# Three layer norms: the modulated activations made on VectorE, their high parts on ScalarE, and three instructions moved

## The chip, the cores and the metric

The kernel runs on one core of one Trainium2 chip. A core has TensorE (PE, matmuls), VectorE (DVE, elementwise), ScalarE (ACT, one-input functions with a scale and a bias for each partition), GpSimd (POOL, which here mostly issues DMAs) and SyncE (SP, DMAs only). The engines run their own instruction streams and wait for each other by semaphores. The metric is device time of one execution in microseconds (us), the median of the runs shown.

## The reference, cut to what matters

The whole computation is two transformer blocks, one after the other, for 512 tokens of width 1024. The first has an attention layer and a gated linear attention layer, each with an MLP. The second has a gated delta net and a retention layer, each followed by a convolutional feed-forward net (FFN). The change touches the second one only, where each of the four sublayers ends in a layer norm:

```
def _standardize(x, eps):
    mu = jnp.mean(xf, axis=-1, keepdims=True)
    xc = xf - mu
    var = jnp.mean(xc * xc, axis=-1, keepdims=True)
    return xc * lax.rsqrt(var + eps)

for i in range(DEPTH):                       # DEPTH = 2
    sh1, sc1, g1, sh2, sc2, g2 = jnp.split(mod, 6, axis=-1)
    y = mixers[i % N_MIXERS_2](x * (1.0 + sc1) + sh1)
    x = layer_norm(DN_ALPHA * x + (1.0 + g1) * y, ln_g[i, 0], ln_b[i, 0])
    y = conv_ffn(x * (1.0 + sc2) + sh2, ffn_up[i], ffn_conv_w[i], ffn_conv_b[i], ffn_down[i])
    x = layer_norm(DN_ALPHA * x + (1.0 + g2) * y, ln_g[i, 1], ln_b[i, 1])
```

What the next product reads is h = x * (1 + sc) + sh, and x itself is normed times gain plus bias. So h is the normed value times one column of numbers plus another, one number of each for every feature.

## The kernel before, in words

Activations lie transposed: `xT[:, b, 256:768]` is block b (0 to 7) of 128 features for the 512 tokens. Large matmuls are done in float32 accuracy from split operands: a value is cut into a rounded high part (fp32r) and the rest, its low part, and a product is three matmuls, high x high, low x high and high x low (`split_product`, L737 records all of them). ACT makes the high parts by writing them in fp32r. DVE makes the low parts by subtraction: `w_lo` for weights (L2335, in two halves of a group), `x_lo` for activations (L2341 and L2344).

The four layer norms are named ln0 (after the delta net), ln0f (after FFN 0), ln1 (after retention) and ln1f (after FFN 1, the last work before the output). Each has two pieces.

- `add_residual` runs over the eight output blocks j of the projection ahead of the norm, as PE finishes them. DVE adds each block to `xT`, centres it around a first mean, and adds the squares that ACT makes (`ln_squares`, L1931) to a sum (`add_squares`, L2715). Between them stand splits of weights: the lists `before` and `after` say behind which block a group is split. At j = 6 it is the group `ffn0_up` 0 for ln0, `ffn1_up` 0 for ln1, and for ln0f and ln1f the last group of the FFN's own down projection, which PE still needs for block 7 (it takes this group from the 12th of its 22 steps on). ACT does the high half of the same group just ahead of squares 6 and 7.
- `layer_norm` follows once the sums over features are there. PE adds up over the partitions by matmuls with ones: `begin_sums` (L796, L798) stands six matmuls ahead of the end of block 7 and takes squares 0 to 6, `end_sums` (L803, L805) takes block 7. ACT makes the reciprocal deviation (`ln_deviation`, L1940 and L1942, semaphore n_std). DVE centres each block once more (`center`, L2763) and multiplies it by the deviation (L2778, semaphore n_mul). For ln0, ln0f and ln1, ACT then makes h in `hT` (L1588) and copies it to its high part (L1561 for ln0 and ln1, which write an array with holes, L1563 for ln0f), and DVE subtracts for the low part (L2341 or L2344), two blocks behind its multiplications. For ln1f there is no next product: ACT applies gain and bias (L1596).

PE's next stage goes block by block over the same eight inputs: for input block k it waits for low part k (`input_split`), then does six matmuls. The first such column of 48 matmuls needs weight group 0, the next one group 1, whose high parts ACT makes behind its last activation of the norm (for ln0 and ln1 behind a load of its function table too), and whose low parts DVE makes behind its last x_lo.

After ln0 there is more. POOL streams the modulation weights `in_ada_w` for the last norms in pieces of 256 KB. Its loop waits for n_mul to reach 40, which is the eighth multiplication of ln0, since a slot of the pieces lies in the deviation's array. DVE weighs four pieces (`mod_piece`, L2163 and L2165) ahead of its split of group 1 of `ffn0_up`, and four behind it.

The order on each engine is that of the code: no planner moves anything. SP loads weight groups into a ring of two slots, each as soon as PE has begun on the group after the one in the slot.

## Time and profile before

| | |
|---|---|
| median of 3 runs | 3748.09 us |
| lowest, highest | 3744.73, 3749.03 us |
| the profiled execution: time, span | 3753.23 us, 3751.5 us |
| PE busy | 3512.0 us, 94% of the span |
| PE weight loads busy | 2820.2 us, 75% |
| DVE busy | 1917.2 us, 51% |
| ACT busy | 1194.3 us, 32% |
| POOL busy | 211.6 us, 6% |
| mean granted TensorE clock | 0.973 of full speed |

Times of rows count from the start of the span. The span is the profiled execution on the core, 1.7 us less than its time. The busy share is an average over some forty stages, so it says that PE is the engine to look at, not what a norm costs. For that one reads the four stretches in which PE waits for a norm or starts the column behind it: about 2463 to 2489 us (ln0), 2863 to 2888 (ln0f), 3339 to 3362 (ln1) and 3726 to 3741 (ln1f).

### The profile page before, as it was taken

Reading aid. Unit: us, or ns where it says so; the run is one execution under the profiler, and the core shown is the slowest. Engines: PE = TensorE matmul, PEld = TensorE weight load, DVE = VectorE, ACT = ScalarE, POOL = GpSimd, SP = SyncE. Lnnn points to the kernel's source line nnn. Section 1 sums busy time; section 2 is a strip of 40 time slices with the busy share of each in tenths; the row PEclk is TensorE's granted clock in tenths of the full one; section 3 lists DMA queues with packets and bytes.
Section 4 is the critical chain, followed back from the end, with each engine's and each line's share of the span. In section 5 each row is a group of like instructions: output and inputs, shape, how many; then the busy total and the mean of one; then the engine's idle time right before and its main releaser. Section 6 shows DMA issues by size and latency. Waiting matters only on the chain.

```text
span 3751.5 us, 45103 instructions
## 1 busy us (share of the span) xinstructions
PE 3512.0 (94%) x17014; PEld 2820.2 (75%) x17014; DVE 1917.2 (51%) x2755; ACT 1194.3 (32%) x1545; POOL 211.6 (6%) x374
## 2 busy tenths in 40 slices
PE   7999889999997998899999999789998999899998
PEld 3566679999995887677846665678877777678876
DVE  4555546445446564644445665577745333454434
ACT  3033424213224342533322333243323222333332
POOL 0111001001000000111100000011100000000000
PEclk9999999999998999999999999899999999999999
DMA  6212114234221111444421111045533222122222
GB/s 209 80 58 65 49 36 133 93 99 127 91 85 41 40 56 56 135 157 154 157 68 35 34 34 45 23 140 181 181 108 101 67 73 73 56 84 96 89 84 84
DMA packets 294723, 335.30 MB, mean 89 GB/s; under 512 B 16465, under 2 KB 264145, under 8 KB 294481
## 3 DMA queue, kind: packets, MB, share of 16 engines
q1 hardware_dynamic: 261552, 232.93, 19.7%
q0 software_dynamic: 29440, 96.49, 8.1%
q10 hardware_dynamic: 3617, 4.26, 0.4%
q8 instruction: 83, 1.36, 0.2%
q14 instruction: 31, 0.25, 0.0%
HBM read 331.55 MB, written 2.10 MB: 89 GB/s over the span
## 4 chain that ended last, share of the span: by engine, by line
PE 86%; DVE 6%; ACT 2%; DMA 2%; issue 2%; ACTq 0%; DVEq 0%; POOL 0%; SPq 0%; POOLq 0%
PE acc L737 64%; PE sc L737 6%; PE sc L1318 2%; DMA wring<-in_mlp_w 1%; PE acc L962 1%; PE sc L878 1%; PE sc L942 1%; PE acc L1318 1%; PE acc L1498 1%; PE sc L944 1%; DVE w_lo L2335 1%; DVE arena L2093 1%; DVE xT L2097 0%; DVE d_col L2284 0%; PE acc L953 0%
## 5 line engine op out<-in xcount | busy, mean ns | idle before, releaser
L737 PE MATMUL acc<-x_lo,w_hi 128*128 128x512 f32 (+1 forms) x2144 | 810.1, 378 | 31.3 <-DVE d_out_lo L2312 9.2
L2335 DVE TENSOR_TENSOR w_lo<-wring,w_hi 128x1024 fp32r<-128x1024 f32 (+2 forms) x400 | 441.7, 1146 | 560.1 <-ACT w_hi L1674 560.1
L1674 ACT ACTIVATE w_hi<-wring 128x1024 fp32r<-128x1024 f32 (+2 forms) x400 | 377.4, 991 | 996.6 <-DMA wring<-in_mlp_w 483.1
L737 PEld LDWEIGHTS acc<-x_lo,w_hi 128*128 128x128 f32 x2144 | 408.5, 191 | 95.4 <-DVE w_lo L2335 25.4
L737 PE MATMUL acc<-hid_hi,w_hi 128*128 128x512 f32 (+1 forms) x1120 | 415.0, 371 | 18.6 <-DVE w_lo L2335 9.3
L737 PE MATMUL acc<-hid_hi,w_lo 128*128 128x512 f32 (+1 forms) x1120 | 410.7, 367 | 0.0
L737 PE MATMUL acc<-x_hi_holes,w_hi 128*128 128x512 f32 x704 | 282.1, 401 | 15.3 <-DVE x_lo L2341 13.9
L737 PE MATMUL acc<-x_hi_holes,w_lo 128*128 128x512 f32 x704 | 278.5, 396 | 0.0
L737 PE MATMUL acc<-hid_lo,w_hi 128*128 128x384 f32 (+1 forms) x768 | 272.2, 354 | 0.0
L737 PEld LDWEIGHTS acc<-hid_hi,w_hi 128*128 128x128 f32 x1120 | 212.0, 189 | 48.0 <-DVE arena L2371 11.8
L737 PE MATMUL acc<-x_hi_seq,w_hi 128*128 128x512 f32 x576 | 228.1, 396 | 16.2 <-DVE x_lo L2344 13.7
L737 PEld LDWEIGHTS acc<-hid_hi,w_lo 128*128 128x128 f32 x1120 | 211.8, 189 | 24.8
L737 PE MATMUL acc<-x_hi_seq,w_lo 128*128 128x512 f32 x576 | 225.2, 391 | 0.0
L737 PE MATMUL acc<-x_hi,w_hi 128*128 128x384 f32 (+1 forms) x608 | 208.6, 343 | 11.2 <-DVE x_lo L2344 6.2
L737 PE MATMUL acc<-x_hi,w_lo 128*128 128x384 f32 (+1 forms) x608 | 207.4, 341 | 0.0
L737 PE MATMUL acc<-wide_lo,w_hi 128*128 128x512 f32 x480 | 188.6, 393 | 0.0
L737 PE MATMUL sc<-hT,wring 128*128 128x512 f32 x384 | 177.7, 606 | 0.5 <-DVE d_col L2561 0.5
L723 POOL DMA_DIRECT2D rows_or_mod<-in_ada_w x176 | 94.9, 539 | 1421.3 <-DVE xT L2778 605.0
L737 PEld LDWEIGHTS acc<-x_hi_holes,w_hi 128*128 128x128 f32 x704 | 133.5, 190 | 48.1 <-issue 16.1
L2165 DVE SCALAR_TENSOR_TENSOR tab<-rows_or_mod,cs,tab 128x512 f32<-128x512 f32 x204 | 147.9, 748 | 30.8 <-DMA rows_or_mod<-in_ada_w 27.4
L737 PEld LDWEIGHTS acc<-x_hi_holes,w_lo 128*128 128x128 f32 x704 | 133.6, 190 | 32.5
L737 PEld LDWEIGHTS acc<-hid_lo,w_hi 128*128 128x128 f32 x768 | 145.0, 189 | 9.8
(416 smaller groups left out, 5930.7 us busy)
## 6 DMA issues: line engine op xcount, KB each, us to landing
wring<-in_mlp_w SPq DMA_DIRECT2D x64, 1024.0 KB, 5.4
rows_or_mod<-in_ada_w POOLq DMA_DIRECT2D x208, 256.0 KB, 3.1
wring<-in_ffn_up SPq DMA_DIRECT2D x44, 1024.0 KB, 5.1
wring<-in_ret_w_in SPq DMA_DIRECT2D x24, 1024.0 KB, 5.2
rstd<-in_ada_w POOLq DMA_DIRECT2D x88, 256.0 KB, 3.4
wring<-in_ffn_down SPq DMA_DIRECT2D x32, 704.0 KB, 4.7
wring<-in_gdn_w_in SPq DMA_DIRECT2D x16, 1024.0 KB, 5.8
tab<-in_ada_w POOLq DMA_DIRECT2D x40, 256.0 KB, 3.4
```

What stands on the lines that cost most here:

```text
L723: pool.dma_start(mod_w[s], w[:, k, bass.ds(it * (per * MOD_N) + i * MOD_N, MOD_N)]).then_inc(mod_loaded[s], 16)
L737: ins = pe.matmul(o, lhsT, rhs, start=start, stop=stop)
L878: last = pe.matmul(mod_psum[:, bass.ds(it * (MOD_PIECES[phase] // DB * per * nv) + c, 1)], mod_acc[:, i % 2, v, m * P:(m + 1) * P], ones[: ...
L942: pe.matmul(sc[:, n % 2, h, 0:w], qn[:, e, t * P:(t + 1) * P], kn[:, e, k0:k0 + w], start=True, stop=False)
L944: last = pe.matmul(sc[:, n % 2, h, 0:w], qr[:, t * P:(t + 1) * P], krope[:, e, k0:k0 + w], start=False, stop=True)
L962: last = pe.matmul(unit(S, 11 + 2 * n)[:, 0, 0:P], vtok[:, k, e * P:(e + 1) * P], probT[:, n % 2, k * P:(k + 1) * P], start=k == 0, stop=k ...
L1318: last = pe.matmul(o[:, e, t], left[:, e, t], right[:, e, t], start=True, stop=True)
L1498: last = pe.matmul(unit(S, 8 + j)[:, i, t * P:SEQ], r_v[:, t, m // CTX, m % CTX:m % CTX + P], r_s[:, t, 0:SEQ - t * P], start=t == 0, stop ...
L1674: f(w_hi[s][:, c], wring[s][:, c], ACT.Copy).then_inc(w_high, 1)
L2093: st.did(tt(y[:, b + 1], y[:, b + 1], rstd[:, 0:n], MUL))
L2165: ins = stt(a, mod_w[s], cs[:, k, v:v + 1], a, MUL, ADD)
L2335: tt(w_lo[s][:, c], wring[s][:, c], w_hi[s][:, c].bitcast(F32), SUB).then_inc(w_split, 1)
```

## The change

Three edits.

1. In `add_residual` at j = 6 the sum takes square 6 (the seventh) ahead of the split of the next weights, in all four norms, where it stood behind it.
2. In `layer_norm` each multiplication stands ahead of the centring of the block three further on, where it stood behind it.
3. For ln0, ln0f and ln1, ACT writes the high part of h from `xT` in one activation with scale and bias, and no longer `hT`. DVE computes `hT` itself by a tensor_scalar (times one column, plus another), one for each block, and subtracts for the low part one block behind, where it was two. The tensor_scalar waits for n_mul, DVE's own multiplication, and the subtraction for h_ready, DVE's own tensor_scalar, besides x_high.

```
--- before.py
+++ after.py
@@ -1585,9 +1585,9 @@
 
                 for b in range(DB):
                     act.wait_ge(n_mul, mul0 + b + 1)
-                    f(hT[:, b, CTX:T], xT[:, b, CTX:T], ACT.Identity, scale=ln_col[:, i, 0, b:b + 1],
-                      bias=ln_col[:, i, 1, b:b + 1]).then_inc(h_ready, 1)
-                    high_input(SEQ, b, h0, holes)
+                    x = xT[:, b, CTX:T]
+                    f(x_hole(b) if holes else x_hi_seq[:, b, :], in_two(x) if holes else x, ACT.Identity,
+                      scale=ln_col[:, i, 0, b:b + 1], bias=ln_col[:, i, 1, b:b + 1]).then_inc(x_high, 1)
 
             def layer_norm_out(l, i, mul0):
 
@@ -2334,9 +2334,13 @@
                     dve.wait_ge(w_high, half_group(stage, it, j, h))
                     tt(w_lo[s][:, c], wring[s][:, c], w_hi[s][:, c].bitcast(F32), SUB).then_inc(w_split, 1)
 
-            def low_input(n, b, x0, holes=False):
+            H0 = 40
+
+            def low_input(n, b, x0, holes=False, h0=None):
 
                 dve.wait_ge(x_high, x0 + b + 1)
+                if h0 is not None:
+                    dve.wait_ge(h_ready, h0 + b + 1)
                 if holes:
                     tt(in_two(x_lo[:, b, CTX:T]), in_two(hT[:, b, CTX:T]), x_hole(b).bitcast(F32), SUB).then_inc(x_split, 1)
                     return
@@ -2745,11 +2749,11 @@
                             st.did(ins)
                         else:
                             ins.then_inc(x_added, 1)
-                    for b in {3: (1,), 4: (2,), 5: (3,), 6: (5,)}.get(j, ()):
+                    for b in {3: (1,), 4: (2,), 5: (3,), 6: (5, 6)}.get(j, ()):
                         add_squares(b)
                     splits(after.get(j, ()))
-                    for b in {5: (4,), 6: (6,)}.get(j, ()):
-                        add_squares(b)
+                    if j == 5:
+                        add_squares(4)
                     if phase and j == 5:
                         dve.wait_ge(mod_summed, 1 + MOD_CHUNKS * (phase + 1))
                         modulation(phase + 1, 0, 6, 1)
@@ -2758,6 +2762,7 @@
             def layer_norm(name, i, x0=None, holes=False, follows=None):
 
                 _, b0, _ = NORMS[name]
+                h0 = H0 + DB * i
 
                 def center(b):
                     st.did(stt(xT[:, b, CTX:T], sc[:, 0, 1, :], -1.0 / D, xT[:, b, CTX:T], MUL, ADD))
@@ -2771,16 +2776,21 @@
                 if follows:
                     split_weights(*follows)
                 deviation_of(name)
+                if x0 is not None:
+                    dve.wait_ge(ln_cols, (1, 3, 3)[i])
                 for b in range(DB):
+                    st.settle(min(2, DB - 1 - b))
+                    tt(xT[:, b, CTX:T], xT[:, b, CTX:T], rstd[:, 0:SEQ], MUL).then_inc(n_mul, 1)
                     if b + 3 < DB:
                         center(b + 3)
-                    st.settle(min(3, DB - 1 - b))
-                    tt(xT[:, b, CTX:T], xT[:, b, CTX:T], rstd[:, 0:SEQ], MUL).then_inc(n_mul, 1)
-                    if x0 is not None and b >= 2:
-                        low_input(SEQ, b - 2, x0, holes)
+                    if x0 is not None:
+                        dve.wait_ge(n_mul, 8 * (4 + i) + b + 1)
+                        ts(hT[:, b, CTX:T], xT[:, b, CTX:T], ln_col[:, i, 0, b:b + 1], ln_col[:, i, 1, b:b + 1],
+                           MUL, ADD).then_inc(h_ready, 1)
+                        if b:
+                            low_input(SEQ, b - 1, x0, holes, h0)
                 if x0 is not None:
-                    low_input(SEQ, DB - 2, x0, holes)
-                    low_input(SEQ, DB - 1, x0, holes)
+                    low_input(SEQ, DB - 1, x0, holes, h0)
 
             def down_residual(i, l, x0):
```

DVE's stream at the end of `add_residual` of ln0f, before. L2715 adds a square to the sum (the one with `rstd` square 5, the other square 6), L2335 splits the last weight group of the down projection (128x704, two halves):

```order
L2743 TENSOR_TENSOR sq<-sq,xT 128x512 [waits dve_step]
L2715 TENSOR_TENSOR sq<-sq,rstd 128x512 [waits n_used,n_sq]
L2335 TENSOR_TENSOR w_lo<-wring,w_hi 128x704 [waits w_high] x2
L2715 TENSOR_TENSOR sq<-sq 128x512 [waits n_used,n_sq]
L2728 SCALAR_TENSOR_TENSOR xT<-acc,dcol,xT 128x512 [waits acc_ready,n_cent]
```

The same place in the changed kernel (line numbers are a few higher):

```order
L2747 TENSOR_TENSOR sq<-sq,xT 128x512 [waits dve_step]
L2719 TENSOR_TENSOR sq<-sq,rstd 128x512 [waits n_used,n_sq]
L2719 TENSOR_TENSOR sq<-sq 128x512 [waits n_used,n_sq]
L2335 TENSOR_TENSOR w_lo<-wring,w_hi 128x704 [waits w_high] x2
L2732 SCALAR_TENSOR_TENSOR xT<-acc,dcol,xT 128x512 [waits acc_ready,n_cent]
```

The add of square 6 with its wait for n_sq, ACT's square, now stands in front of both halves of the split.

DVE's stream at the start of `layer_norm` of ln0, before, from the centrings of blocks 0 to 2 on. L2763 centres, L2778 multiplies, L2341 makes a low part:

```order
L2763 SCALAR_TENSOR_TENSOR xT<-sc,xT 128x512 x3
L2763 SCALAR_TENSOR_TENSOR xT<-sc,xT 128x512 [waits n_std]
L2778 TENSOR_TENSOR xT<-xT,rstd 128x512 [waits dve_step]
L2763 SCALAR_TENSOR_TENSOR xT<-sc,xT 128x512
L2778 TENSOR_TENSOR xT<-xT,rstd 128x512 [waits dve_step]
L2763 SCALAR_TENSOR_TENSOR xT<-sc,xT 128x512
L2778 TENSOR_TENSOR xT<-xT,rstd 128x512 [waits dve_step]
L2341 TENSOR_TENSOR x_lo<-hT,x_hi_holes 128x512 [waits x_high]
```

In the changed kernel L2768 centres, L2783 multiplies, L2788 is the new tensor_scalar and L2345 makes a low part:

```order
L2768 SCALAR_TENSOR_TENSOR xT<-sc,xT 128x512 x3
L2783 TENSOR_TENSOR xT<-xT,rstd 128x512 [waits dve_step,ln_cols,n_std]
L2768 SCALAR_TENSOR_TENSOR xT<-sc,xT 128x512
L2788 TENSOR_SCALAR hT<-xT,ln_col 128x512 [waits n_mul]
L2783 TENSOR_TENSOR xT<-xT,rstd 128x512 [waits dve_step]
L2768 SCALAR_TENSOR_TENSOR xT<-sc,xT 128x512
L2788 TENSOR_SCALAR hT<-xT,ln_col 128x512 [waits n_mul]
L2345 TENSOR_TENSOR x_lo<-hT,x_hi_holes 128x512 [waits h_ready,x_high]
```

Ahead of the first multiplication stand three centrings instead of four. Ahead of the first low part stand five centrings, two multiplications and two tensor_scalars, where there were six centrings and three multiplications.

The end of the same norm and what follows it on DVE, before. The low parts 5, 6 and 7 stand behind the last multiplication; L2163 and L2165 weigh modulation pieces, and `w_lo1` is group 1 of `ffn0_up`:

```order
L2778 TENSOR_TENSOR xT<-xT,rstd 128x512 [waits dve_step]
L2341 TENSOR_TENSOR x_lo<-hT,x_hi_holes 128x512 [waits x_high] x3
L2844 MEMSET sq 128x2x2
L2832 UNCONDITIONAL_BRANCH
L2832 ISA
L2159 ISA [waits mod_summed]
L2163 TENSOR_SCALAR tab<-rows_or_mod,cs 128x512 [waits mod_loaded0]
```

And in the changed kernel, from the seventh multiplication on:

```order
L2783 TENSOR_TENSOR xT<-xT,rstd 128x512 [waits dve_step]
L2788 TENSOR_SCALAR hT<-xT,ln_col 128x512 [waits n_mul]
L2345 TENSOR_TENSOR x_lo<-hT,x_hi_holes 128x512 [waits h_ready,x_high]
L2783 TENSOR_TENSOR xT<-xT,rstd 128x512 [waits dve_step]
L2788 TENSOR_SCALAR hT<-xT,ln_col 128x512 [waits n_mul]
L2345 TENSOR_TENSOR x_lo<-hT,x_hi_holes 128x512 [waits h_ready,x_high] x2
L2854 MEMSET sq 128x2x2
```

The last multiplication now has six low parts and seven tensor_scalars in front of it, where it had five low parts. The streams of PE, SP and POOL are the same in both kernels. ACT's loses the second of its two activations for each of 24 blocks.

## Rows read from the trace of the kernel before

**Rows 1.** The page's part on the chain that ended last, shares of the span.
```profile
PE 86%; DVE 6%; ACT 2%; DMA 2%; issue 2%; ACTq 0%; DVEq 0%; POOL 0%; SPq 0%; POOLq 0%
```
**Rows 2.** Timeline of DVE, ln0: start us, length us, engine, line, operation.
```profile
2457.35 0.68 DVE L2715 TENSOR_TENSOR sq<-sq,rstd 128x512 f32<-128x512 f32 x1
...
2469.52 0.68 DVE L2778 TENSOR_TENSOR xT<-xT,rstd 128x512 f32<-128x512 f32 x1
...
2472.52 0.68 DVE L2341 TENSOR_TENSOR x_lo<-hT,x_hi_holes 128x512 fp32r<-128x512 f32 x1
...
2479.14 0.68 DVE L2778 TENSOR_TENSOR xT<-xT,rstd 128x512 f32<-128x512 f32 x1
...
2487.41 2.36 DVE L2335 TENSOR_TENSOR w_lo<-wring,w_hi 128x1024 fp32r<-128x1024 f32 x2
```
**Rows 3.** Timeline of ACT, ln0.
```profile
2457.13 0.61 ACT L1931 ACTIVATE sq<-xT 128x512 f32<-128x512 f32 x1
...
2470.30 0.81 ACT L1588 ACTIVATE hT<-xT,ln_col 128x512 f32<-128x512 f32 x1 [1.67 <-DVE xT L2778]
```
**Rows 4.** Timeline of PE, ln0; in brackets the idle time and its releaser.
```profile
2459.25 1.02 PE L796 MATMUL sc<-sq,base_tab 128*128 128x512 f32 x2
2460.96 1.12 PE L798 MATMUL sc<-sq,base_tab 128*128 128x512 f32 x2 [0.69 <-DVE sq L2715]
...
2473.35 0.77 PE L737 MATMUL acc<-x_hi_holes,w_hi 128*128 128x512 f32 x1 [6.96 <-DVE x_lo L2341]
...
2488.69 0.50 PE L737 MATMUL acc<-x_hi_holes,w_hi 128*128 128x512 f32 x1 [1.40 <-DVE w_lo L2335]
```
**Rows 5.** Timeline of POOL behind ln0.
```profile
2480.64 1.13 POOL L723 DMA_DIRECT2D rows_or_mod<-in_ada_w  x2 [604.99 <-DVE xT L2778]
```
**Rows 6.** Timeline of DVE, first MLP: two tensor_scalars back to back.
```profile
577.18 0.88 DVE L2163 TENSOR_SCALAR tab<-rows_or_mod,cs 128x512 f32<-128x512 f32 x2
```
**Rows 7.** Timeline of DVE: ln0f, ln1, and a wait for its own result.
```profile
2871.44 0.68 DVE L2778 TENSOR_TENSOR xT<-xT,rstd 128x512 f32<-128x512 f32 x1
...
3344.91 0.68 DVE L2778 TENSOR_TENSOR xT<-xT,rstd 128x512 f32<-128x512 f32 x1
...
3359.63 2.36 DVE L2335 TENSOR_TENSOR w_lo<-wring,w_hi 128x1024 fp32r<-128x1024 f32 x2 [1.67 <-ACT w_hi L1674]
...
3364.63 2.97 DVE L2815 SCALAR_TENSOR_TENSOR arena<-sq,cols,arena 128x512 f32<-128x512 f32 x4 [0.17 <-DVE arena L2813]
```
**Rows 8.** Timeline of ACT: ln0f, ln1, ln1f.
```profile
2852.79 0.62 ACT L1931 ACTIVATE sq<-xT 128x512 f32<-128x512 f32 x1
...
3357.25 1.28 ACT L1534 ACT_TABLE_LOAD   x1
...
3716.07 0.61 ACT L1931 ACTIVATE sq<-xT 128x512 f32<-128x512 f32 x1
```
**Rows 9.** The chain that ended last, FFN 1's down projection: start us, length us, what.
```profile
3708.35 0.90 DVE w_lo L2335
```
**Rows 10.** Timeline of PE: FFN 0's down projection, then columns behind ln0f, ln1, then ln1f.
```profile
2744.17 0.79 PE L737 MATMUL acc<-hid_hi,w_hi 128*128 128x512 f32 x1 [4.65 <-DVE w_lo L2335]
...
2853.75 0.39 PE L737 MATMUL acc<-hid_hi,w_hi 128*128 128x512 f32 x1
...
2859.88 1.03 PE L796 MATMUL sc<-sq,base_tab 128*128 128x512 f32 x2
2860.74 1.02 PE L798 MATMUL sc<-sq,base_tab 128*128 128x512 f32 x2
...
2887.71 0.39 PE L737 MATMUL acc<-x_hi_seq,w_hi 128*128 128x512 f32 x1
...
3361.87 0.40 PE L737 MATMUL acc<-x_hi_holes,w_hi 128*128 128x512 f32 x1
...
3723.08 1.02 PE L796 MATMUL sc<-sq,base_tab 128*128 128x512 f32 x2
```
**Rows 11.** Stretch of PE: from:to, us, busy (count), granted clock, DMA share, GB/s.
```profile
2744.10:2748.10 4.00, 3.93 (x9) 0.50 0.43 117
```

## The prediction, made before the changed kernel ran

> **What bounds the kernel now.** I read the chain that ended last first: 86% of the span is PE, 6% DVE [rows 1]. So an instruction elsewhere counts only where PE waits for it, and I went on to the timelines of PE, DVE and ACT around the four layer norms, where it does. In ln0 the reader is to see three waits of PE. It stands 0.69 us ahead of L798, for DVE's add of square 6 (`sq`, L2715). It stands 6.96 us until the first low part, and 1.40 us behind the first column of the next product, for the low weights of group 1 [rows 4]. In between PE is fed without a gap. In ln0f and ln1 the 49th matmul of the next product follows the first column without a wait, at 2887.71 and 3361.87 [rows 10]. So between the first low part and the last, DVE has some room, and the question is how much of it the change uses up.
>
> **DVE's pace through a norm.** From the first multiplication, 2469.52, to the first low part, 2472.52, lie five steps, so a step of 512 columns costs 0.60 us [rows 2]; the length of 0.68 us includes an end that overlaps the next start. The trace has the new tensor_scalar in other places: two take 0.88 us, which with the same overlap of 0.08 is a step of 0.40 and a length of 0.48 [rows 6]. I take 0.40. Its bounds are 0.40 and the 0.60 of the other steps; at 0.60 each of three norms would be some 1.5 us longer than below. A wait for its own last result costs more than a step: DVE stood 0.17 us between L2813 and L2815 [rows 7], where back-to-back work has an overlap of 0.08. I take 0.12 for it, between 0 and 0.25. It counts for blocks 5, 6 and 7 only, where the tensor_scalar stands right behind its multiplication; in blocks 0 to 4 a centring stands between.
>
> The Trainium skill speaks against that wait having a price (VectorE: DVE Perf Modes, section "The DRAIN you can't avoid": chained instructions with a semaphore after each take as long as without, so that the semaphore adds nothing). The 0.17 us disagrees [rows 7]. By the page the norm would lose two waits of 0.12 less in each of three norms, and the sum below would be 0.7 us smaller.
>
> Counted from the first multiplication, the changed order is: block 0 multiplication, centring, tensor_scalar, 1.60; blocks 1 to 4 with a low part too, 2.20 each, so multiplication 5 starts at 10.40; blocks 5 and 6 multiplication, wait, tensor_scalar, low part, 1.72 each. So multiplication 7 starts at 13.84, low part 6 at 14.96 and low part 7 at 15.56. Before, multiplication 7 started at 2479.14 - 2469.52 = 9.62 [rows 2]. DVE's work between the two grows by 4.22 us.
>
> **ln0.** Square 6 was ready at 2457.13 + 0.61 = 2457.74 [rows 3], and the add of square 5 starts at 2457.35 [rows 2], so the moved add starts about 2458.1 and ends by 2458.9. L798 can then follow L796 by the 0.86 us that the two stand apart in ln0f (2859.88 to 2860.74) [rows 10], at 2460.11 and not 2460.96 [rows 4]: a gain of 0.85. The split behind it ends near 2461.1, before DVE gets block 7, so it costs nothing. Moving the multiplication ahead of the fourth centring gains one step, 0.60. ACT's second activation goes, but what it hid behind is DVE: an activation starts 0.78 behind its multiplication and takes 0.81 [rows 2, 3], so a high part is there 1.59 behind it and only the last is even near its low part. That edit gains nothing by itself.
>
> Multiplication 7 starts at 2479.14 - 0.85 - 0.60 + 4.22 = 2481.91, 2.77 later. POOL waits for that multiplication alone, and issued its first piece 1.50 behind it [rows 2, 5]. Four pieces are weighed ahead of the split of group 1, which starts 8.27 behind multiplication 7, and PE 1.28 behind that [rows 2, 4]. POOL, the transfers and DVE's weighing all move along, so PE's 2488.69 becomes 2491.46: **+2.77**.
>
> PE's first column ends earlier than that. PE starts 0.83 behind a low part (2472.52 to 2473.35) [rows 2, 4]. A block needs six matmuls, 0.23 us apart at full clock (2853.75 to 2859.88 are 27 of them) [rows 10], so 1.38 a block, and the lows now come 2.20 and then 1.72 apart: the column becomes bound by DVE. Its last two blocks start with low part 6, at 15.79, and take 2.76: end at 18.55 behind the first multiplication. In ln0 that is 2486.6, so PE then idles for 4.8 us. At 2744.17 it had idled 4.65, and the granted clock was 0.50, the 1.2 GHz level, over the next 4.00 us, with 9 matmuls in them [rows 10, 11]. Nine at full clock take 2.1, so the fall costs **+1.9**; its bounds are 0 and that.
>
> **ln0f.** The moved add waits for square 6, which ACT makes behind the high weights of the group that DVE is to split. It is ready at 2852.79 + 0.62 = 2853.41 [rows 8]. The add starts at 2853.44, the split one step behind at 2854.04, and PE has the first half 0.90 + 0.13 later [rows 9], at 2855.07. PE wants it for step 12 of block 7, the 27th matmul ahead of L796, at 2853.75 [rows 10]. It had it in time and now waits **+1.32**. Bounds are 0 and 1.5.
>
> The first multiplication moves from 2871.44 [rows 7] to 2870.84, and the column ends at 2870.84 + 18.55 = 2889.39, against 2887.71 [rows 10]: **+1.68**. The low weights of group 1 are split by then.
>
> **ln1.** PE does not wait at L798 here, so the moved add gains nothing and delays only a split wanted much later. The first multiplication goes from 3344.91 [rows 7] to 3344.31. The column would end at 3362.86. But ACT's last activation ends at 13.84 + 1.59 = 15.43, the table load takes 1.28 [rows 8], the split starts 1.10 behind the load (3358.53 to 3359.63) [rows 7, 8], and PE 1.28 behind that: 19.1 in all, 3363.4 against 3361.87 [rows 10]: **+1.55**.
>
> **ln1f.** Square 6 is ready at 3716.68 [rows 8], so PE has the half at 3718.34 and wants it 6.13 ahead of 3723.08, at 3716.95 [rows 10]: **+1.39**. Behind the sums the norm has the same steps up to its last multiplication, in another order: nothing, within 0.2.
>
> **The sum.** 2.77 + 1.9 + 1.32 + 1.68 + 1.55 + 1.39 = 10.6 us. FFN 0, retention and FFN 1 behind these places are PE without gaps in the chain, so nothing is given back. On the profiled execution, 3753.23 us, that is 3763.8. This execution lies 5.1 above the median of the runs shown, in what the change doesn't touch, so I put the sum on the median: 3748.09 + 10.6 = **3758.7 us**.
>
> **Rivals.**
> - The clock does not fall in ln0. It needs PE's idle 4.8 us to do less than the 4.65 at 2744. Then 3758.7 - 1.9 = 3756.8.
> - ln0's delay is taken up: pieces land sooner or a later wait in FFN 0 hides it, so that only the column counts there. For it: eight pieces stand around the split, and not all need be bound by POOL. Against: the chain goes through them. Then ln0 costs nothing, and 10.6 - 4.7 = 5.9 gives 3754.0.
> - The clock falls in the starved columns. PE is busy 1.38 of each 2.20 us there. If the last twelve matmuls in ln0f and ln1 run at 0.44 and not 0.23, that is 2.5 each: 3763.7. Against: single waits of 1.40 left the rate as it was [rows 4].
> - The other side, not slower: the column's start decides. The first low part comes 0.4 us sooner in three norms (3.20 instead of 3.00 behind a multiplication 0.60 earlier), and in ln0 0.85 more: 2.0 us off, 3746.1. It decides from the point where DVE needs no more than 1.38 us a block, and the stalls in the down projections are covered. The rows give 2.20 and 1.72.
> - The change doesn't do what it says (all of it lies beside other work): 3748.1.
>
> **How the numbers follow.** My forecast 0.45, clock stays up 0.17, ln0's delay taken up 0.15, starved clock 0.13, start decides 0.05, nothing 0.05. The measurement can tell about 0.2% from no change, 7.5 us, so slower begins at 3755.6. Slower takes most of the forecast (0.40), most of the second (0.12), the fourth (0.13) and a little of the third (0.03): 0.68. Faster gets 0.04, the same 0.28. The range for 8 in 10 reaches down to the third case, less one for the spread of runs, 3753, and up to the starved clock, or to a tensor_scalar of 0.60 us, 3764.
>
> **What would show it.** In the changed profile: L798 0.86 behind L796 in ln0; tensor_scalars of 0.48 us; multiplication 7 13.8 us behind the first in three norms; PE waiting for x_lo inside the first column; a wait of about 4.8 us for w_lo in ln0 with the clock at 0.5 behind it; a PE wait of 1.3 in block 7 of both down projections, for w_lo. The prediction is wrong if tensor_scalar takes no time of its own, if PE is fed through the column without gaps, or if the split's half is there before PE wants it.

## The result, and the profile after

| | before | changed |
|---|---|---|
| median of 6 runs each, us | 3746.43 (3741.69 to 3752.7) | 3763.35 (3757.78 to 3769.14) |
| profiled execution, us | 3753.23 | 3761.88 |
| its span, us | 3751.5 | 3760.2 |
| mean granted clock | 0.973 | 0.973 |
| ratio, 95% interval | | 1.0041 (1.0031 to 1.0052) |

The changed kernel is slower, by 15.4 us by the ratio and 16.9 between the medians. A second comparison with five rounds (e11 below) gave 1.0025 (1.0015 to 1.0034), 9.4 us. The forecast was 3758.7, which is 10.6 above the median then known, 3748.09.

The two spans differ by 8.7 us only. Of the 8.2 us between that and the difference of the medians, 3.1 lie in code ahead of the change. The output projection of the delta layer, ahead of ln0, starts at 2413.11 in the trace of before and at 2409.98 in that of the changed kernel. The rest is within what single executions differ by: those of the changed kernel lie between 3757.78 and 3769.14. Over all the kernels below the same point lies between 7.4 us earlier and 2.4 us later than before. So one span against another tells little at this size. I read the change from that point on, in one trace against one other: from there to the output's first matmul (L1521) the changed kernel takes 7.75 + 3.13 = **10.9 us** more.

**ln0.** The timeline of PE in the changed kernel; columns as in [rows 4].

```profile
2456.15 1.02 PE L796 MATMUL sc<-sq,base_tab 128*128 128x512 f32 x2
2457.01 1.02 PE L798 MATMUL sc<-sq,base_tab 128*128 128x512 f32 x2
...
2469.00 0.77 PE L737 MATMUL acc<-x_hi_holes,w_hi 128*128 128x512 f32 x1 [6.68 <-DVE x_lo L2345]
...
2475.69 0.50 PE L737 MATMUL acc<-x_hi_holes,w_hi 128*128 128x512 f32 x1 [0.61 <-DVE x_lo L2345]
...
2477.55 0.49 PE L737 MATMUL acc<-x_hi_holes,w_hi 128*128 128x512 f32 x1 [0.20 <-DVE x_lo L2345]
...
2488.86 0.80 PE L737 MATMUL acc<-x_hi_holes,w_hi 128*128 128x512 f32 x1 [4.75 <-DVE w_lo L2335]
```

The wait ahead of L798 is gone: it follows L796 by 0.86, where it followed by 1.71 [rows 4]. PE now waits inside the first column for low parts, first at its fourth block. Behind the long wait the granted clock is at the 1.2 GHz level, so the first matmuls of the column stand 0.43 apart and not 0.23: eight of them here, 13 before. The wait for the low weights of group 1 is 4.75 us and was 1.40 [rows 4].

DVE in the same place, to be set beside [rows 2]; the POOL row answers to [rows 5].

```profile
2464.86 0.68 DVE L2783 TENSOR_TENSOR xT<-xT,rstd 128x512 f32<-128x512 f32 x1
...
2466.06 0.54 DVE L2788 TENSOR_SCALAR hT<-xT,ln_col 128x512 f32<-128x512 f32 x1
2466.51 0.69 DVE L2783 TENSOR_TENSOR xT<-xT,rstd 128x512 f32<-128x512 f32 x1
...
2475.55 0.69 DVE L2783 TENSOR_TENSOR xT<-xT,rstd 128x512 f32<-128x512 f32 x1
2476.27 0.55 DVE L2788 TENSOR_SCALAR hT<-xT,ln_col 128x512 f32<-128x512 f32 x1
...
2479.12 0.69 DVE L2783 TENSOR_TENSOR xT<-xT,rstd 128x512 f32<-128x512 f32 x1
...
2483.86 0.49 DVE L2163 TENSOR_SCALAR tab<-rows_or_mod,cs 128x512 f32<-128x512 f32 x1 [2.26 <-DMA rows_or_mod<-in_ada_w]
...
2487.59 2.35 DVE L2335 TENSOR_TENSOR w_lo<-wring,w_hi 128x1024 fp32r<-128x1024 f32 x2
```

```profile
2480.62 1.13 POOL L723 DMA_DIRECT2D rows_or_mod<-in_ada_w  x2 [610.23 <-DVE xT L2783]
```

From the first multiplication to the last lie 2479.12 - 2464.86 = 14.26 us; it was 9.62. A tensor_scalar moves DVE on by 0.45 (2466.06 to 2466.51). Where it stands right behind its multiplication it starts 0.72 later instead of 0.60. The 4.64 us more are seven tensor_scalars (3.2), a sixth low part (0.6) and a fifth centring (0.6) between the two multiplications, and two waits of DVE for its own result (0.24). The centring had stood ahead of the first multiplication, so its 0.6 is no loss.

POOL issues 1.50 behind the last multiplication, as before, and the split of group 1 starts 8.47 behind it (before 8.27). In between DVE stands idle for the first piece, in both kernels (above 2.26 us, and here in the trace of before):

```profile
2483.77 0.49 DVE L2163 TENSOR_SCALAR tab<-rows_or_mod,cs 128x512 f32<-128x512 f32 x1 [1.21 <-DMA rows_or_mod<-in_ada_w]
```

So the way from the last multiplication to PE goes through POOL's issue and the landing of the pieces.

The stretch of 4 us from PE's restart on: time, busy, matmuls, granted clock, DMA share, GB/s. The first row is of the changed kernel, the second of the kernel before at the same place.

```profile
2488.80:2492.80 4.00, 3.94 (x9) 0.50 0.77 240
```

```profile
2488.60:2492.60 4.00, 3.91 (x17) 1.00 0.70 226
```

Nine matmuls instead of seventeen: the granted clock is at the 1.2 GHz level.

**ln0f, ln1 and ln1f.** PE again; these answer to [rows 10].

```profile
2855.97 0.50 PE L737 MATMUL acc<-hid_hi,w_hi 128*128 128x512 f32 x1 [1.12 <-DVE w_lo L2335]
...
2877.34 0.76 PE L737 MATMUL acc<-x_hi_seq,w_hi 128*128 128x512 f32 x1 [8.95 <-DVE x_lo L2348]
...
2885.90 0.47 PE L737 MATMUL acc<-x_hi_seq,w_hi 128*128 128x512 f32 x1 [0.22 <-DVE x_lo L2348]
...
2892.24 0.39 PE L737 MATMUL acc<-x_hi_seq,w_hi 128*128 128x512 f32 x1
...
3369.59 0.50 PE L737 MATMUL acc<-x_hi_holes,w_hi 128*128 128x512 f32 x1 [0.25 <-DVE w_lo L2335]
...
3724.68 0.49 PE L737 MATMUL acc<-hid_hi,w_hi 128*128 128x512 f32 x1 [1.03 <-DVE w_lo L2335]
```

The first and the last row are the two waits in block 7 of the down projections. The column starts at 2877.34 and not 2875.27, and the 49th matmuls stand at 2892.24 and 3369.59, where they stood at 2887.71 and 3361.87 [rows 10]. DVE shows what PE waits for in block 7:

```profile
2854.42 0.69 DVE L2719 TENSOR_TENSOR sq<-sq 128x512 f32<-128x512 f32 x1 [4.26 <-ACT sq L1931]
2855.03 1.69 DVE L2335 TENSOR_TENSOR w_lo<-wring,w_hi 128x704 fp32r<-128x704 f32 x2
```

The moved add waits for ACT's square, and the split waits behind it.

### The profile page after: what moved, and what is told of

Its sections match the earlier page's. It is cut to its first block, busy times and chain, and to the rows that moved or that the text cites. A ratio compares the mean times of both kernels' runs of the same rounds, so it can differ in the third digit from the quotient of the medians.

```text
span 3760.2 us, 45131 instructions
## 1 busy us (share of the span) xinstructions
PE 3517.8 (94%) x17014; PEld 2820.6 (75%) x17014; DVE 1929.4 (51%) x2779; ACT 1180.3 (31%) x1521; POOL 211.6 (6%) x374
## 4 chain that ended last, share of the span: by engine, by line
PE 86%; DVE 7%; ACT 3%; DMA 2%; issue 2%; ACTq 0%; DVEq 0%; SPq 0%; POOL 0%; POOLq 0%
PE acc L737 64%; PE sc L737 6%; PE sc L1318 2%; PE acc L962 1%; PE sc L878 1%; DMA wring<-in_mlp_w 1%; PE sc L942 1%; PE acc L1318 1%; PE acc L1498 1%; PE sc L944 1%; DVE w_lo L2335 1%; DVE xT L2783 0%; DVE d_col L2284 0%; DVE arena L2093 0%; PE acc L953 0%
## 5 line engine op out<-in xcount | busy, mean ns | idle before, releaser
L2335 DVE TENSOR_TENSOR w_lo<-wring,w_hi 128x1024 fp32r<-128x1024 f32 (+2 forms) x400 | 441.9, 1146 | 556.8 <-ACT w_hi L1674 556.5
L2165 DVE SCALAR_TENSOR_TENSOR tab<-rows_or_mod,cs,tab 128x512 f32<-128x512 f32 x204 | 147.9, 748 | 31.3 <-DMA rows_or_mod<-in_ada_w 27.9
```

Of the source, the lines that this page charges most:

```text
L2165: ins = stt(a, mod_w[s], cs[:, k, v:v + 1], a, MUL, ADD)
L2335: tt(w_lo[s][:, c], wring[s][:, c], w_hi[s][:, c].bitcast(F32), SUB).then_inc(w_split, 1)
```

## The experiments

Each kernel was timed in five rounds beside the kernel before. "Shift" is the start of an instruction less that of the same one in the trace of before; "local" is the shift at the output less the shift at 2413.11, all in us.

| kernel | ratio (95%) | shift 2413.11 | group 1 behind ln0 | ln0f L803 | 49th behind ln0f | 49th behind ln1 | output | local |
|---|---|---|---|---|---|---|---|---|
| change | 1.0041 (1.0031 to 1.0052) | -3.13 | +0.17 | +2.36 | +4.53 | +7.72 | +7.75 | 10.9 |
| e11 | 1.0025 (1.0015 to 1.0034) | +0.53 | +3.72 | +5.50 | +7.66 | +9.65 | +9.00 | 8.5 |
| e1 | 1.0002 (0.9993 to 1.0012) | -2.54 | -3.84 | -1.15 | -0.27 | +0.39 | -0.68 | 1.9 |
| e2 | 1.0003 (0.9994 to 1.0013) | -7.42 | -7.05 | -6.47 | -5.16 | -4.17 | -6.65 | 0.8 |
| e3 | 1.0030 (1.0021 to 1.0039) | +2.42 | +7.19 | +8.40 | +11.19 | +14.41 | +14.68 | 12.3 |
| e4 | 1.0024 (1.0015 to 1.0034) | -4.55 | -1.10 | +1.34 | +3.50 | +6.52 | +4.95 | 9.5 |
| e8 | 1.0058 (1.0044 to 1.0071) | +0.24 | +6.37 | +9.01 | +14.83 | +21.09 | +20.90 | 20.7 |
| e9 | 1.0016 (1.0005 to 1.0026) | +0.79 | +0.24 | +2.55 | +4.72 | +8.27 | +8.28 | 7.5 |
| e12 | 0.9993 (0.9984 to 1.0002) | -4.17 | -5.11 | -4.27 | -4.72 | -4.25 | -7.01 | -2.8 |

The shifts inside a norm repeat well from trace to trace, the local sums to some 2 us only (the change and e11, the same kernel: 10.9 and 8.5). One reason is in the table. From behind ln1 to the start of FFN 1's down projection (3608.39 in the trace of before) the shift falls by 2.1 to 2.3 in e1, e2, e4, e8, e9, e11 and e12, and stays within 0.1 in the change and in e3. So that stretch was slow in three traces (before, the change, e3) and quick in seven. No kernel differs in it, and PE's one wait, at its end, is 3.63 to 3.67 us in all ten. The 2.1 us spread evenly over it: in the three traces the matmuls stand 0.2331 us apart, in the seven 0.2310, at a granted clock of 1.00 in both. This drops out of the sums of the change and e3. In the others it makes the sum 2.1 smaller: e11 would have 10.6, e1 4.0, e2 2.9, e4 11.6, e8 22.8, e9 9.6 and e12 -0.7.

Two stretches of the down projections, from their first matmul (2744.17, 3608.39) to L796 of the norm, and the one from group 1 to 2744.17, are read over all traces too; the entry is by how much the shift grows. Under the first two stand PE's waits inside them, summed, and the mean granted clock there:

| | change | e11 | e1 | e8 | e9 | e2 | e3 | e4 | e12 |
|---|---|---|---|---|---|---|---|---|---|
| add 6 ahead of the split in ln0f, ln1f | yes | yes | yes | yes | yes | no | no | no | no |
| 2744.17 to L796 of ln0f | 0.35 | 0.03 | 2.76 | 0.63 | 2.15 | -1.01 | -1.19 | 0.38 | 1.01 |
| PE's waits in it (before 0.34) | 1.12 | 1.08 | 1.94 | 1.32 | 1.92 | 0.16 | 0 | 0.16 | 0.73 |
| clock in it (before 0.980) | 0.988 | 0.986 | 0.976 | 0.987 | 0.977 | 0.987 | 0.985 | 0.974 | 0.974 |
| 3608.39 to L796 of ln1f | 0.02 | 1.59 | 1.17 | 1.86 | 2.23 | -0.13 | 0.18 | 0.67 | -0.54 |
| PE's waits in it (before 0.64) | 1.03 | 1.71 | 1.65 | 1.41 | 1.43 | 0.55 | 0 | 0.62 | 0.16 |
| clock in it (before 0.985) | 0.986 | 0.985 | 0.987 | 0.976 | 0.975 | 0.986 | 0.977 | 0.977 | 0.987 |
| granted clock fell behind ln0 | yes | yes | no | yes | no | no | yes | yes | no |
| group 1 to 2744.17 | 1.83 | 1.75 | -0.08 | 2.01 | 0.16 | 1.59 | 2.40 | 2.06 | -0.18 |

Each of the two down projections starts behind a wait of PE (4.65 at 2744.17, 3.67 at 3608.39 in the trace of before), and how long the granted clock then stays at 0.50 differs from trace to trace, whatever the kernel. A mean clock lower by 0.01 over 115 us is some 1.2 us. The difference in waits and the difference in clock together give the growth of every entry within 0.6 us. So the wait in block 7 is what the early add does, and the clock is most of the scatter.

**e1, e2, e3: each edit by itself.** e1 is before with `{..., 6: (5, 6)}` and the add of square 6 no longer behind the splits. e2 is before with

```
                 for b in range(DB):
+                    st.settle(min(2, DB - 1 - b))
+                    tt(xT[...], xT[...], rstd[...], MUL).then_inc(n_mul, 1)
                     if b + 3 < DB:
                         center(b + 3)
-                    st.settle(min(3, DB - 1 - b))
-                    tt(xT[...], xT[...], rstd[...], MUL).then_inc(n_mul, 1)
```

and e3 is the change with both of these undone.

> Edit 1 alone (square 6 ahead of the split, in all four norms). My theory: in ln0 L798 follows L796 0.86 us behind (a gain of 0.85), and PE waits about 1.1 us for w_lo in block 7 of both down projections, since the split now waits for ACT's square 6; together about +1 us, with the waits to be seen in the profile. Rival: the order of the add is a pure gain, no wait in block 7, -0.9 us.

> Edit 2 alone (each multiplication ahead of the centring). My theory: first multiplication 0.60 us nearer to the sums, multiplication 7 where it was, so PE starts its column 0.6 us sooner in three norms and keeps that in ln0f and ln1 only: -1.2 us. Rival: the earlier start is what DVE's order is worth in ln0 too, -1.8 us and more, by an earlier rise of the clock.

> Edit 3 alone (high parts written from xT, hT by a tensor_scalar on DVE, low parts one block behind). My theory: DVE's pace is the cost. Multiplication 7 lies 14.3 us behind the first instead of 9.6, so group 1 of ffn0_up comes 4.6 us later and the clock falls in the wait (+1.9), and the first columns behind ln0f and ln1 end 2.7 us later each: about +12 us. Rival: most of the change's loss is in the order of the add and of the multiplications, and this alone costs under 5 us.

e1 did at its four places what was expected. In ln0 L798 comes at once. In the down projections PE waits for the split that is held:

```profile
2456.65 1.02 PE L796 MATMUL sc<-sq,base_tab 128*128 128x512 f32 x2
2457.50 1.02 PE L798 MATMUL sc<-sq,base_tab 128*128 128x512 f32 x2
...
2852.46 0.50 PE L737 MATMUL acc<-hid_hi,w_hi 128*128 128x512 f32 x1 [1.25 <-DVE w_lo L2335]
...
3716.14 0.50 PE L737 MATMUL acc<-hid_hi,w_hi 128*128 128x512 f32 x1 [1.23 <-DVE w_lo L2335]
```

The whole time can't be told from no change: 1.0002, and its interval reaches to 1.0012, which would be 4.5 us.

e2 gained nothing, and here my expectation of 0.6 per norm failed. The timeline of DVE in ln0f:

```profile
2864.36 0.69 DVE L2776 TENSOR_TENSOR xT<-xT,rstd 128x512 f32<-128x512 f32 x1
...
2867.96 0.69 DVE L2344 TENSOR_TENSOR x_lo<-hT,x_hi_seq 128x512 fp32r<-128x512 f32 x1
```

The first low part stands 3.60 behind the first multiplication; before it was 3.00 [rows 2]. The multiplication moved ahead by one step and the low part did not, because in either order six centrings and three multiplications stand ahead of it. PE waits 9.24 for it, as in e1, where the order is the old one.

e3 by itself loses about as much as the whole change: 1.0030, with an interval that meets those of both comparisons, and a local sum of 12.3 where some 12 were expected.

**e4: the add of square 6 early in ln0 and ln1 only.** The change with

```
+                    early = 6 if name in ("ln0", "ln1") else None
...
+                    if j == early:
+                        add_squares(6)
                     splits(after.get(j, ()))
```

> The changed kernel with square 6 behind the split again for ln0f and ln1f, ahead of it for ln0 and ln1 as in the change. My theory: the two waits in block 7 (1.12 and 1.03 us) are gone and a wait of some 0.6 that a DMA sets may be back before the second: 1.5 to 2.2 us under the changed kernel, about +13 on the kernel before. Rival: PE waits there anyway (for the weights' DMA), no difference to the changed kernel.

Both block-7 waits are gone. PE's waits in the two stretches are 0.16 and 0.62 (the latter for another half group, at 3684.45), where the change has 1.12 and 1.03. But the stretches grow by 0.38 and 0.67, no less than the change's 0.35 and 0.02: the granted clock was 0.974 and 0.977 in them in this trace, and 0.988 and 0.986 in that of the change. The ratio is 1.0024 beside 1.0025 and 1.0041 for the change: the intervals meet, so the whole time does not show what the trace does. Against the kernel before it is 9 us, where 13 were expected.

**e9: ln0 with the high part from hT again.** The change with, for i == 0 only,

```
+                    if i == 0:
+                        f(hT[...], x, ACT.Identity, scale=..., bias=...).then_inc(h_ready, 1)
+                        high_input(SEQ, b, h0, holes)
+                        continue
```

on ACT, and on DVE no tensor_scalar and the low parts two blocks behind.

> The changed kernel with edit 3 undone for ln0 alone (ACT writes hT and copies it, no tensor_scalar, low parts two blocks behind). My theory: multiplication 7 is 4.6 us sooner and PE's wait behind the first column is short again, so no fall of the clock there: 6.5 us under the changed kernel. Rival: ln0 costs no more than the other two norms, 2.2 us.

PE in ln0, and the four microseconds from its restart on:

```profile
2473.38 0.76 PE L737 MATMUL acc<-x_hi_holes,w_hi 128*128 128x512 f32 x1 [6.97 <-DVE x_lo L2350]
...
2488.93 0.50 PE L737 MATMUL acc<-x_hi_holes,w_hi 128*128 128x512 f32 x1 [2.60 <-DVE w_lo L2340]
```

```profile
2488.80:2492.80 4.00, 3.87 (x17) 1.00 0.79 230
```

The wait is 2.60 and the clock stays up. From 2413.11 to 2744.17 the shift goes from +0.79 to +0.40. In the change it goes from -3.13 to +2.00, and in e11 from +0.53 to +5.47: ln0 costs 5.1 and 4.9 with edit 3 there, and -0.4 without, so nothing of it was given back in FFN 0. The ratio moved from 1.0025 or 1.0041 to 1.0016, the right way. Its interval meets that of e11 and not that of the first comparison. The expected 6.5 us under the change are between 3.4 and 9.4 by the ratios, so the whole time does not size ln0's part.

**e8: two tensor_scalars.** The change with one more of the same kind ahead of each, written to a scratch tile:

```
+                        ts(sq_total, xT[:, b, CTX:T], ln_col[:, i, 0, b:b + 1], ln_col[:, i, 1, b:b + 1],
+                           MUL, ADD)
                         ts(hT[:, b, CTX:T], xT[:, b, CTX:T], ...)
```

> The changed kernel with a second tensor_scalar of the same form and size in front of the first, 24 more in all, which writes an array that nothing reads any more. My theory, DVE's pace: each costs 0.45 us, seven of them stand ahead of multiplication 7 and of low part 6, so ln0, ln0f and ln1 each end 3.2 us later: +9.5 on the changed kernel. Rival: DVE has room (51% busy over the span) and the loss of the change is in its order: under +2.

DVE in ln0, the first block and the last:

```profile
2468.11 0.68 DVE L2783 TENSOR_TENSOR xT<-xT,rstd 128x512 f32<-128x512 f32 x1
...
2469.31 0.54 DVE L2788 TENSOR_SCALAR sq<-xT,ln_col 128x512 f32<-128x512 f32 x1
2469.77 0.54 DVE L2790 TENSOR_SCALAR hT<-xT,ln_col 128x512 f32<-128x512 f32 x1
2470.22 0.69 DVE L2783 TENSOR_TENSOR xT<-xT,rstd 128x512 f32<-128x512 f32 x1
...
2485.57 0.68 DVE L2783 TENSOR_TENSOR xT<-xT,rstd 128x512 f32<-128x512 f32 x1
```

Two back to back are 0.46 apart, and the last multiplication stands 17.46 behind the first: 3.20 more than with one, seven times 0.46. PE follows in all three norms. From L803 to the matmul behind the column the shift grows by 7.19 in ln0 (change 4.24), 5.82 in ln0f (change 2.17) and 5.17 in ln1 (change 1.93): 2.95, 3.65 and 3.24 more. By the ratio e8 is 21.8 us above the kernel before, so 6.4 or 12.4 above the change, and by the local sums 9.8 or 12.2; 9.5 was expected. The waits inside the first column grew with it; the one at group 1 did not (4.06), since the column itself ended later:

```profile
2481.22 0.50 PE L737 MATMUL acc<-x_hi_holes,w_hi 128*128 128x512 f32 x1 [0.80 <-DVE x_lo L2345]
...
2483.54 0.49 PE L737 MATMUL acc<-x_hi_holes,w_hi 128*128 128x512 f32 x1 [0.67 <-DVE x_lo L2345]
...
2495.06 0.50 PE L737 MATMUL acc<-x_hi_holes,w_hi 128*128 128x512 f32 x1 [4.06 <-DVE w_lo L2335]
```

**e5 and e7: group 1's split ahead of the four pieces.** If the four pieces that stand ahead of the split are what holds PE in ln0, the split can go first. e5 is the change, e7 the kernel before with edits 1 (in ln0 and ln1) and 2, both with

```
-                    pieces(0)
                     split_weights(up, it, 1)
+                    pieces(0)
                     pieces(4)
```

> The changed kernel with DVE splitting group 1 of ffn0_up ahead of the first four modulation pieces and not behind them. My theory: PE's 4.75 us wait for w_lo behind ln0 comes by way of multiplication 7, POOL and the four pieces; with the split in front it shrinks to about 0.4 and the clock doesn't fall there. PE then meets the pieces themselves (L878, the modulation sum, in the middle of column 1) and the next group, whose splits are unmoved, so that only some 2 us of the 6.6 are left as a gain. Rival: the wait is for ACT's high parts of group 1 (late behind its last activation and the table load), then the 4.75 stays above 3.

> The kernel before with square 6 ahead of the split in ln0 and ln1 only, multiplications ahead of the centrings, and group 1 of ffn0_up split ahead of the modulation pieces. My theory: 0.85 us from L798 in ln0, the 1.40 us wait behind its first column turned into one at the modulation sum, nothing from the multiplications (the first low part has nine instructions in front of it either way): -1 to -2 us on the kernel before, too little to be told from no change. Rival: all three are gains, -3 us and more.

Both are far slower: e5 1.0239 (1.0225 to 1.0253), e7 1.0198 (1.0184 to 1.0212). The waits of PE from 2480 to 2730, in e5 and in the change (total, times, longest):

```profile
PE sc L878 <- DVE tab L2165: 34.6, 8, 6.1
PE acc L737 <- DVE w_lo L2335: 0.2, 1, 0.2
```

```profile
PE acc L737 <- DVE w_lo L2335: 4.8, 1, 4.8
```

The wait for the split in ln0 is gone, as meant. But this order stands in a loop, and in every pass the sum at L878 now waits for the table's pieces: over the whole run 11 waits, 45.3 us, that neither kernel had. The mean granted clock went from 0.973 to 0.965, which over 3760 us is some 30 more (0.008 of it). The two are some 75. Less the 4.75 at group 1 that are gone, and the 3.4 by which this trace is ahead of the change's already at 2413.11, that leaves 67 of the 68.5 us between the spans. Even the pass where the split was late gains nothing: its own wait at L878 is the longest, 6.1 us, and the 4.75 are all that it saves. The other ten passes had nothing to save.

**e11: the change again**, with no edit.

> The changed kernel once more, unedited, to size its loss. From the parts, measured apart, edit 3 costs 11 to 12 us, edit 1 about 1 to 2 with its gain in ln0 inside, edit 2 nothing: my theory of four places expects +11 to +12 on the kernel before. Rival: the first comparison's +15 to +17 holds, and something outside the four norms is slower too.

1.0025. The places in its trace are those of the first: waits of 0.59 and 0.21 inside the column and 4.54 at group 1, the granted clock 0.50 over the 4 us behind it with 9 matmuls, 1.09 in block 7 of FFN 1.

**e12: the direct high part for the first block only.** PE's start wants one low part early, and seven tensor_scalars buy nothing for it. The kernel before with the early add in ln0 and ln1, the multiplication first, and ACT's direct form and DVE's tensor_scalar for block 0 only. In ln0 the last three multiplications, for the last of which POOL waits, go ahead of low parts 3 to 7 (m multiplication, c centring, t tensor_scalar, l low part):

```
+    order = "m0 c3 t0 m1 l0 c4 m2 c5 l1 m3 c6 m4 l2 c7 m5 m6 m7 l3 l4 l5 l6 l7"         (ln0)
+    order = "m0 c3 t0 m1 l0 c4 m2 c5 l1 m3 c6 l2 m4 c7 l3 m5 l4 m6 l5 m7 l6 l7"     (ln0f, ln1)
```

> The kernel before with what the runs left standing: square 6 ahead of the split for ln0 and ln1 only; multiplication 0 ahead of centring 3; the high part written directly and hT made by DVE for block 0 alone; and in ln0 the last three multiplications ahead of low parts 3 to 7. My theory: L798 0.85 us sooner and multiplication 7 9.45 instead of 10.22 us behind the last of the first three centrings, so 1.6 us in ln0; PE's column starts 1.3 us sooner behind ln0f and ln1 and ends 0.9 to 1.2 us sooner, being supplied by ACT at the end: -3.7 us. Rival: the earlier start is eaten up inside the columns, -1.6 us or less.

It took 3747.9, the kernel before 3750.5 in the same runs and the change (e11) 3759.9. So it is some 12 us faster than the change and can't be told from the kernel before. PE in ln0:

```profile
2467.05 0.77 PE L737 MATMUL acc<-x_hi_holes,w_hi 128*128 128x512 f32 x1 [5.62 <-DVE x_lo L2346]
...
2474.77 0.51 PE L737 MATMUL acc<-x_hi_holes,w_hi 128*128 128x512 f32 x1 [1.11 <-DVE x_lo L2346]
...
2483.58 0.50 PE L737 MATMUL acc<-x_hi_holes,w_hi 128*128 128x512 f32 x1 [1.60 <-DVE w_lo L2340]
```

The column starts 1.3 us sooner (a wait of 5.62 and not 6.96 [rows 4]). But the fourth block then waits 1.11, since its low part stands behind the last three multiplications in this order, and group 1 again waits for its low weights. DVE was done with the last low part sooner, and stood for a piece instead:

```profile
2479.97 0.75 DVE L2170 SCALAR_TENSOR_TENSOR tab<-rows_or_mod,cs,tab 128x512 f32<-128x512 f32 x1 [1.33 <-DMA rows_or_mod<-in_ada_w]
```

Of the column's start little reaches its end. In ln0 the matmul behind the column comes 0.94 sooner, most of it by the early L798; in ln0f it is 0.45, and in ln1 it comes 0.05 later. I had expected 1.6, 0.9 and 1.2.

## Why the prediction was right

The forecast of 10.6 us stands beside 15.4 and 9.4 in two comparisons and 10.9 and 8.5 in two traces. The median of 3763.35 lies just inside the upper end of the range, 3764, and the base had moved: over six runs it is 3746.43 and no longer 3748.09. So the sign and the mechanism were right, and the size lies between what the two comparisons give. The forecast's own steps, each in the trace of the changed kernel:

- **L798 in ln0**: 0.85 expected, 0.85 seen.
- **DVE's pace.** 13.84 us from the first multiplication to the last were expected, 14.26 seen. The term that was off is the tensor_scalar. I took a step of 0.40 from the two of [rows 6], which have one form of operand; the one here, with two columns of `ln_col`, takes a step of 0.45 and a length of 0.54. Seven times 0.05 to 0.06 is the 0.42. It lies at the near end of the bounds of 0.40 and 0.60. The wait for its own result costs 0.12, as taken: 0.72 from start to start (2475.55 to 2476.27) beside 0.60. The Trainium skill (VectorE: DVE Perf Modes, section "The DRAIN you can't avoid") has it that a semaphore after each instruction costs nothing extra. In this trace that holds for raising one: the multiplication raises n_mul, and the centring behind it starts 0.60 later (2464.86 to 2465.46). Waiting for the instruction directly ahead does cost here, 0.12 each time.
- **ln0 to group 1**: +2.77 expected, +3.27 seen (L796 3.10 earlier, group 1 0.17 later). The 0.42 of the pace is most of the 0.50.
- **The clock**: +1.9 expected, +1.83 seen between group 1 and FFN 0's down projection, with the granted clock at 0.50 and nine matmuls in 4 us, as at 2744 [rows 11]. The five traces with the fall have 1.75 to 2.40 here. Three of the four without it have nothing; e2 has 1.59, of which 0.7 are waits for low weights.
- **ln0f's held split**: a wait of 1.32 expected, 1.12 seen (1.25 in e1). The square came as worked out. All five traces with the early add have this wait, 1.08 to 1.32, and none of the others has it. PE's waits in the whole stretch are 1.48 in the mean of the five and 0.28 in the other five: 1.2 more. The net in the change's trace is 0.35 only, since the granted clock of the stretch was 0.988 in it and 0.980 in the trace of before, which is some 0.8 us back by no doing of the change.
- **ln0f's column**: +1.68 expected, +2.17 seen, the pace once more.
- **ln1**: +1.55 expected, +1.93 seen, bound where it was said, by the split behind the last activation and the table load.
- **ln1f's held split**: a wait of 1.39 expected, 1.03 seen (1.03 to 1.43 over the five). PE's waits in the stretch are 1.45 in the mean of the five and 0.39 in the others: 1.1 more. In the change's trace the net is 0.02. Before, PE had stood 0.64 for another half group (3709.38), and that wait was not there. In other traces such a wait stands beside it (e11: 0.40 and 1.09), so this was no exchange that the change makes.

The terms that were sized too small (ln0, ln0f's column, ln1) come to 1.4 together, nearly all by DVE's pace.

That the trace's 10.9 is so near to 10.6 is in part luck. The two held splits, 2.7 in the forecast, are 0.4 net in this trace. And 1.3 us came where the forecast has no term: from 2887.71 to L796 of ln1 at 3335.63, through the retention layer, the shift grows by 1.26. PE's waits there are 21.9 us in both traces, but the granted clock is 0.989 in the change's and 0.992 in that of before. e4, e8 and e9 have 0.989 too and grow by 1.1 to 1.6. e11, the same kernel as the change, has 0.992 and grows by 0.05. So this is scatter.

One premise was wrong as written. The forecast gave nothing back because PE runs "without gaps" in FFN 0, retention and FFN 1. It does not: it stands 4.65 at 2744.17, 21.9 in all in the retention layer and 3.67 at 3608.39. These waits are as long in the changed kernel (4.62, 21.9, 3.67), so they move along with what comes before, and the conclusion holds. The 1.38 a block for the first column is also too little for its first blocks, at the 1.2 GHz level. That changed nothing, since the column's end hangs on low part 6.

The rivals. **The clock stays up** is refuted by the window at 0.50. **ln0's delay is taken up** is refuted twice: nothing of it is gone at 2744.17 (shift from +0.17 up to +2.00), and e9, where its cause is taken out, is without it there (+0.40). **The starved columns run slow** did not happen: behind waits of 0.61 and 0.20 in the column the matmuls go on at 0.23 apart. **The column's start decides** had its small truth: the first low part comes 0.28 sooner relative to L803 and PE's column starts sooner, and this is lost at its end, as e12 shows with 1.3. **Nothing** is refuted by both intervals.

Shown by runs: that the direct high parts with their tensor_scalars carry the loss (e3 by itself 1.0030; e1 and e2 can't be told from no change), that DVE's added steps reach PE one for one (e8), and that the early add costs a wait of 1.0 to 1.4 us in each down projection (e1, and gone in e4). What that wait is worth in whole time is not shown, being smaller than the intervals. Not settled: why the two comparisons of one kernel stand 6 us apart. Their intervals, 1.0031 to 1.0052 and 1.0015 to 1.0034, overlap only narrowly, and the spread of some 10 us at 2413.11, ahead of all that was changed, is of that size, as are the 2.1 us ahead of FFN 1's down projection. Part of the scatter goes with the granted clock. Of the 68 executions of the kernel before that stand beside the experiments, the 7 with a mean clock of 0.974 took 3746.3 us in the mean, the 17 with 0.973 took 3748.2 and the 28 with 0.972 took 3751.2. Of the executions of the change, four of six in the first comparison have 0.971, and three of ten in e11. What sets the clock in one execution or the other, and the closer or wider pace of the matmuls at a clock of 1.00, stays open.

## What to carry to other kernels

Where PE follows a chain of blocks from another engine, count two things apart: when the first block arrives, and how far apart the blocks come against what PE needs for one. Here low parts came 2.26 and then 1.79 us apart where PE needs 1.38 at full clock (some 2.6 in its first matmuls behind a long wait, at 0.43 apart); before they came three steps (1.8) and at the end two (1.2) apart. Moving an operation from an engine with room (ACT) to the pacing one (DVE) made the first block come sooner and still lost. Of the 4.6 us by which DVE's norm grew, PE paid 4.2 in ln0, where group 1 hangs on the last multiplication, and 2.2 and 1.9 in ln0f and ln1, where DVE had had some room. Once that room was used up, the next 3.2 (e8) were paid in full. An order in the body of a loop is paid in every pass: look at all of them, not at the one with the visible wait.

## What the runs showed of the hardware

- A tensor_scalar of 128x512 fp32 with two column operands took 0.54 us and a step of 0.45 to 0.46. The two of [rows 6] took 0.88 together, a step of 0.40 and a length of 0.48.
- DVE's next instruction starts 0.08 ahead of the end of the one before. If it must wait for a semaphore of that one, it starts 0.03 behind the end: 0.72 instead of 0.60 from start to start.
- Matmuls of 128x512 in an unbroken stretch stood 0.2331 us apart in three traces and 0.2310 in seven, all at a granted clock of 1.00: 2.1 us over the 247 from 3361.87 to 3608.39.
- The clock fell behind nearly the same idle in two ways. In the change and in e11 (4.75 and 4.54 us of idle) the granted clock was down before PE restarted. In e8 it was still up at the restart behind 4.06 us and fell only afterwards:

```profile
2495.00:2496.00 1.00, 0.94 (x4) 1.00 0.81 258
...
2497.00:2498.00 1.00, 1.00 (x4) 0.50 0.54 117
...
2500.00:2501.00 1.00, 1.00 (x6) 1.00 1.07 351
```

  Idle of 2.60 (e9) and 1.60 (e12) left it at 1.00.
